# Attention: four max columns turned by one matmul, and the sinks' product in FP32r on a rounded and a remainder row

## What is computed

```python
def forgetting_attention(q, k, v, f_logit):
    ...
        s = jnp.einsum('bhqd,bhkd->bhqk', qb, kh) * scale
        s = s + cb[..., None] - cum[:, :, None, :]
        s = jnp.where(causal, s, -jnp.inf)
        p = jax.nn.softmax(s, axis=-1)
        return jnp.einsum('bhqk,bhkd->bhqd', p, vh)

def sliding_window_sink_attention(q, k, v, sinks):
    ...
    s = jnp.where(mask, s, -jnp.inf)
    # sink: each head's learned logit, broadcast to s.shape[:-1] + (1,)
    p = jax.nn.softmax(jnp.concatenate([s, sink], axis=-1), axis=-1)[..., :-1]
    out = jnp.einsum('bnhgqs,bnshd->bnqhgd', p, vv)
```

## Time and profile before

| what | value |
|---|---|
| median of 3 runs | 3542.21 us (3535.03 to 3544.0) |
| span of the profiled execution, first to last instruction | 3534.2 us |
| TensorE busy | 3215.7 us, 91% |
| VectorE busy | 2204.2 us, 62% |
| ScalarE busy | 1407.9 us, 40% |
| mean granted TensorE clock | 0.961 |

### The profile page before, as it was taken

The page is one execution under the profiler, slowest core; times in us unless marked ns, Lnnn a source line. Parts: engine busy times, 40 slices in busy tenths (PEclk is TensorE's granted clock), DMA queues, the critical chain, the costliest instruction groups (busy, mean ns, idle before and its releaser), DMA issues. The chain is left out here.

```text
span 3534.2 us, 43584 instructions
## 1 busy us (share of the span) xinstructions
PE 3215.7 (91%) x15232; PEld 2466.9 (70%) x15232; DVE 2204.2 (62%) x4305; ACT 1407.9 (40%) x2383; POOL 895.6 (25%) x828
## 2 busy tenths in 40 slices
PE   4999999889999997997889999997896899999798
PEld 4799888656666665876667887886784566666576
DVE  7111011267767776332389998995773689998766
ACT  5000001134444445212258998342554233333454
POOL 0111111257455460000421333344231211211000
PEclk9999999899999998998899999998998899999999
DMA  5322223466555533436311335364133523422444
GB/s 208 105 82 73 86 83 118 127 137 144 120 130 114 115 83 118 133 122 236 79 42 44 101 110 175 107 174 157 72 115 116 163 57 70 97 62 54 130 147 134
DMA packets 331916, 400.80 MB, mean 113 GB/s; under 512 B 100324, under 2 KB 249188, under 8 KB 319124
## 3 DMA queue, kind: packets, MB, share of 16 engines
q1 hardware_dynamic: 260376, 299.09, 29.7%
q10 hardware_dynamic: 67488, 78.03, 7.2%
q0 software_dynamic: 3840, 20.98, 2.5%
HBM read 265.39 MB, written 132.62 MB: 113 GB/s over the span
## 5 line engine op out<-in xcount | busy, mean ns | idle before, releaser
L2229 PE MATMUL f_pO<-f_PT,f_vv 128*128 128x512 f32 (+3 forms) x944 | 377.2, 481 | 19.7 <-ACT f_PT L2259 19.7
L2259 ACT ACTIVATE f_PT<-f_pS 128x512 f32<-128x512 f32 (+3 forms) x472 | 221.2, 472 | 325.3 <-PE f_pS L2197 152.8
L2890 DVE TENSOR_SCALAR_CACHE_REDUCE sharedI<-xI,TI 128x768 bf16<-128x768 f32 (+10 forms) x276 | 339.5, 1296 | 5.4 <-DVE TI L2896 5.2
L2694 PE MATMUL cbank<-hT_high,cw_hi 128*128 128x512 f32 x800 | 319.7, 400 | 19.9 <-DVE cw_lo L2849 6.8
L2259 ACT ACTIVATE n_PT<-n_pS 128x512 f32<-128x512 f32 (+4 forms) x352 | 176.6, 504 | 363.0 <-PE n_pS L2209 199.2
L583 PE MATMUL p_bank<-hT_high,p_w_hi 128*128 128x512 f32 (+1 forms) x768 | 304.9, 397 | 16.1 <-DVE p_w_lo L706 16.1
L2694 PE MATMUL cbank<-hT_low,cw_hi 128*128 128x512 f32 x800 | 316.7, 396 | 0.0
L2694 PE MATMUL cbank<-hT_high,cw_lo 128*128 128x512 f32 x800 | 316.3, 395 | 0.0
L2229 PE MATMUL n_pO<-n_PT,n_vv 128*128 128x512 f32 (+4 forms) x704 | 308.3, 519 | 0.0
L583 PE MATMUL p_bank<-hT_low,p_w_hi 128*128 128x512 f32 (+1 forms) x768 | 303.6, 395 | 0.0
L583 PE MATMUL p_bank<-hT_high,p_w_lo 128*128 128x512 f32 (+1 forms) x768 | 302.7, 394 | 0.0
(11 more groups left out here) (421 smaller groups left out, 7412.9 us busy)
## 6 DMA issues: line engine op xcount, KB each, us to landing
f_zz<-scratch_z ACTq DMA_DIRECT2D x128, 128.0 KB, 3.1
c_w_first<-in_w_in_dram SPq DMA_DIRECT2D x26, 512.0 KB, 4.5
cw_raw<-in_w_in_dram SPq DMA_DIRECT2D x25, 512.0 KB, 4.4
p_w_raw<-in_w_in_dram SPq DMA_DIRECT2D x22, 512.0 KB, 3.8
lent<-scratch_qkb POOLq DMA_DIRECT2D x40, 256.0 KB, 10.3
scratch_z<-p_stage ACTq DMA_DIRECT2D x32, 256.0 KB, 2.4
scratch_qk_high<-p_stage ACTq DMA_DIRECT2D x32, 256.0 KB, 2.6
scratch_qk_low<-p_stage_low ACTq DMA_DIRECT2D x32, 256.0 KB, 3.2
```

Of the source, the lines that this page charges most:

```text
L2229: pe.matmul(pO[:, B % 2, c0:c1], lhsT=vv[0:nk, b, kt, :], rhs=PT[0:nk, u % PR, c0:c1], start=(kt == 0 and not heads[h].local), stop=(heads ...
L2259: act.activation(PT[0:nk, u % PR, c0:c1], pS[0:nk, u % SR, c0:c1], ACT.Exp, scale=0.125).then_inc(s_ex, 1)
L2694: last = pe.matmul(bank[:, p % RING, 0:wd], lhsT=w_part[pw][b][:, c, :], rhs=rhs, start=(c == 0 and a == 0), stop=(c == DC - 1 and a == 2))
L2890: own_.up(v.tensor_scalar(junk_v[:, own_.at % 2, 0:(i + 1) * P], scores(i), T[:, j:j + 1], None, compare, ALU.add, accum_out=count[:, j:j ...
```

## The change

The four max columns go into one 128x128 tile, columns 0, 32, 64 and 96, so that one matmul turns them, onto partitions 0, 32, 64 and 96. ScalarE then moves four rows of 128 to row 96 of `QA`, from one partition each, instead of one piece of 32 partitions.

The sink's product becomes FP32r. So that no digits are lost, ScalarE computes the exponential twice, once in full FP32 (`es_full`) and once rounded (`es`, row 96), a new VectorE instruction, `sink_remainder`, writes the difference of the two to row 64 of `es`, and `only` has ones in rows 64 and 96. VectorE waits for ScalarE's pair, and the sink's product waits for VectorE.

```diff
-        Mx = m.sb(n_("Mx"), [P, 4, P], F32R)
+        Mx = m.sb(n_("Mx"), [P, P], F32R)
+        Mx_columns = Mx[:].rearrange("p (r c) -> p r c", r=4)[:, :, 0]
...
-            es = m.sb(n_("es"), [P, 2, QB4])
-            only = m.sb(n_("only"), [P, P])
+            es = m.sb(n_("es"), [P, 2, QB4], F32R)
+            es_full = m.sb(n_("esfull"), [P, QB4])
+            only = m.sb(n_("only"), [P, P], F32R)
...
+                step(gp.memset(only[64:65, HD:P].bitcast(F32), 1.0))
...
-                for r in range(4):
-                    last = pe.matmul(pR[:, r], lhsT=Mx[:, r], rhs=ident_r[:], start=True, stop=True)
-                last.then_inc(s_tr, 1)
+                pe.matmul(pR[:, 0], lhsT=Mx[:], rhs=ident_r[:], start=True, stop=True).then_inc(s_tr, 1)
...
-                act.activation(QA[h % NB][96:P, j * QB4:(j + 1) * QB4], pR[96:P].rearrange("p a b -> p (a b)"), ACT.Copy
-                               ).then_inc(s_mr, 1)
+                for r in range(4):
+                    at = j * QB4 + r * P
+                    last = act.activation(QA[h % NB][96:97, at:at + P], pR[32 * r:32 * r + 1, 0], ACT.Copy)
+                last.then_inc(s_mr, 1)
...
+                    if n:
+                        act.wait_ge(s_es, n)
                     act.wait_ge(s_mr, B + 1)
-                    act.activation(es[96:P, n % 2], QA[h % NB][96:P, j * QB4:(j + 1) * QB4].bitcast(F32), ACT.Exp,
-                                   bias=snk[96:P, heads[h].sink:heads[h].sink + 1], scale=-0.125).then_inc(s_es, 1)
+                    top = QA[h % NB][96:97, j * QB4:(j + 1) * QB4].bitcast(F32)
+                    for to in (es_full[96:97], es[96:97, n % 2]):
+                        last = act.activation(to, top, ACT.Exp, bias=snk[96:97, heads[h].sink:heads[h].sink + 1], scale=-0.125)
+                    last.then_inc(s_eh, 1)
...
+            def sink_remainder(B):
+                n = sink_no[B]
+                v.wait_ge(s_eh, n + 1)
+                v.tensor_tensor(es[64:65, n % 2], es_full[96:97], es[96:97, n % 2].bitcast(F32), ALU.subtract).then_inc(s_es, 1)
...
+                if u in sw.unit0[:-1] and sw.unit0.index(u) in sink_no:
+                    sink_remainder(sw.unit0.index(u))
```

More of the change, by code:

```diff
@@ L1858, in stage_attend @@
             s_snk = m.sem(n_("sinks_loaded"))
-            s_es = m.sem(n_("sink_exponentials"))
+            s_eh, s_es = m.sem(n_("sink_exponentials")), m.sem(n_("sink_remainders"))
         lower, upper = slice(0, HD), slice(HD, P)
@@ L2011, in _ @@
             if local_no:
-                step(gp.memset(es[:], 0.0))
-                step(gp.memset(only[:], 0.0))
-                step(gp.memset(only[96:97, HD:P], 1.0))
+                step(gp.memset(es[:].bitcast(F32), 0.0))
+                step(gp.memset(only[:].bitcast(F32), 0.0))
+                step(gp.memset(only[64:65, HD:P].bitcast(F32), 1.0))
+                step(gp.memset(only[96:97, HD:P].bitcast(F32), 1.0))
             gp.sem_inc(s_const, 1)
@@ L2353, in max_columns @@
                     n = sink_no[B]
-                    own_.up(v.tensor_tensor(Mx[:, :, 96], mxc[:, B % 2, :, 0],
+                    own_.up(v.tensor_tensor(Mx_columns, mxc[:, B % 2, :, 0],
                                             snk8[:, heads[h].sink:heads[h].sink + 1].to_broadcast([P, 4]), ALU.max))
@@ L2361, in max_columns @@
                     a, b = min(r for r, p in runs if p == n), max(r for r, p in runs if p == n) + 1
-                    last = v.tensor_reduce(Mx[:, a:b, 96], mxc[:, B % 2, a:b, 0:n], AX.X, ALU.max)
+                    last = v.tensor_reduce(Mx_columns[:, a:b], mxc[:, B % 2, a:b, 0:n], AX.X, ALU.max)
                 last.then_inc(s_stat, 1)
+            def sink_remainder(B):
+                n = sink_no[B]
+                v.wait_ge(s_eh, n + 1)
+                v.tensor_tensor(es[64:65, n % 2], es_full[96:97], es[96:97, n % 2].bitcast(F32), ALU.subtract).then_inc(s_es, 1)
             def weight(B):
```

## The result

The changed kernel takes 3550.03 us (median of 6 runs, 3548.7 to 3555.68), beside it the kernel before 3541.72 us (6 runs, 3533.82 to 3544.0): ratio 1.0027, with an interval of 1.0015 to 1.0039. It is slower by 5 to 14 us. The forecast was 3541; the range 3528 to 3556 holds the result, but the forecast said no change that can be told, and there is one. One of the 12 executions of the kernel of experiment 10 took 10096.54 us, the other 11 took 3528 to 3544; it is in no ratio.

What follows compares the result with a forecast made beforehand. TensorE and VectorE were taken to set the pace by turns, with GpSimd's loads and a late gate ending VectorE's half. Terms -14.8 - 5.0 + 4.1 + 9.5 + 4.8 = -1.4 us on 3542.2 gave 3541, range 3528 to 3556.

Steps and rivals of the forecast that it cites:

- What bounds the kernel: Both attentions: TensorE and VectorE set the pace in turn, VectorE in local heads, beside a chain of GpSimd and its loads.
- The turn: One turning matmul for four saves 0.36 us where TensorE sets the pace: 14.8 us in first attention, 5.0 in second.
- Copies and FP32r product at nothing: Four small ScalarE copies per block are covered, and the sink's faster product lies in VectorE stretches: both counted 0.
- The remainder's price: VectorE's subtraction in local heads: 0.69 us alone, 1.3 beside GpSimd; three of a head's four beside it, 4.6 us in all.
- each pair loses between 1.4 and 2.5 us; I take 1.9: Five later local-plus-plain head pairs of the first attention: remainders partly absorbed by idle time and slack, +9.5 us in all.
- nothing is absorbed: Far end for the five pairs: each loses the full 4.1 us of remainders, 20.5 us in all.
- The first local head: First attention's first local head, with no late gate behind it: remainders cost +4.1 us.
- The tail: Last two local heads: seven remainders in the chain without GpSimd, +4.8 us, at most 8 if ScalarE's pair is late.
- The clock: TensorE's granted clock, 1.00 in both halves of a pair's period; a fall there would show the prediction wrong.
- The sinks' three terms: Remainder costs in the first attention: first local head +4.1, five pairs +9.5, last two heads +4.8 us.
- the first rival: Whole kernel: turn's gain and remainders' cost cancel, within 10.6 us of before, bounds -13 to +16; chance 0.66.
- the third's: Rival: VectorE's stretch becomes each pair's longer chain; slower once a remainder costs over 0.95 us, up to +22, 3564; chance 0.15.

Runs made afterwards that it cites:

- experiment 10: Changed kernel with GpSimd's raw loads in the five pairs waiting until the plain head's first gate has landed; ratio 0.998 to the kernel before, 3534 us.
- experiments 1 and 3: Kernel before with only the one-matmul turn and small copies, 0.9922; that kernel plus FP32r sink product on rounded exponentials without remainder, 0.9934 (ratios to before).
- experiment 7: Changed kernel with the sink's two exponentials asked for two steps earlier, remainder where it was; ratio 1.0027 to the kernel before.

## Why the prediction was wrong

- **What bounds the kernel**: right in the main. VectorE sets the pace in every local head. In the third pair's local head it is busy 28.69 of 29.47 us after the change, 23.59 of 24.60 with the turn alone. Here are these two, then the same head before, and with the sink's change alone:

```profile
1007.61:1037.08 29.47, 22.45 (x122) 16.32 (x120) 28.69 (x59) 15.69 (x42) 26.90 (x38) 1.00 0.44 99
```

```profile
997.80:1022.40 24.60, 22.88 (x125) 16.86 (x124) 23.59 (x55) 14.29 (x39) 23.65 (x34) 1.00 0.45 110
```

```profile
1001.94:1027.51 25.57, 23.33 (x131) 17.46 (x130) 24.55 (x55) 12.96 (x29) 24.62 (x37) 1.00 0.45 103
```

```profile
1016.84:1046.09 29.25, 23.47 (x129) 17.25 (x127) 28.45 (x61) 14.47 (x32) 26.80 (x38) 1.00 0.44 100
```

- **The turn** (-14.8 and -5.0, -19.8 together): about right by size, not by place. By the ratios it is -16.6 beside the sinks, -19.1 with the gate out of the way and -27.6 (-23 to -32) alone. By the traces the second attention gave 3.6 us on average. The first gave 8.3 alone, 10.2 with the gate out of the way and 16.5 beside the sinks, half of the 10.2 in the pairs' local heads, where none was counted. Why these differ so much is not shown; in the turn-alone trace three plain heads were at the lower clock and gained nothing.
- **Copies and FP32r product at nothing**: right as far as can be told (experiments 1 and 3).
- **The remainder's price**: 28.3 us in all. The forecast's prices were 0.69 alone and 1.3 beside GpSimd; in a pair one of four was long, not three (0.71, 0.69, 1.39, 0.69: 3.5 us, where 4.6 was forecast). What was missed is that work put in between also moves its neighbours to other moments of GpSimd's work. In the third pair's local head the products of `finish` take 1.31 us with the turn alone and 2.50 after:

```profile
997.80:1022.40 24.60, 1.31 (x3) 1.00 0.45 110
```

```profile
1007.61:1037.08 29.47, 2.50 (x3) 1.00 0.44 99
```

So 3.5 us of remainders and 1.2 of `finish` make up the 4.5 that a local head grew by, within 0.2. Before, `finish` took 2.3 us there: its length depends on what of GpSimd's it falls beside, so that each move of the steps changes it, that of a one-input maximum too (1.81 us).
- **The step that failed**: "each pair loses between 1.4 and 2.5 us; I take 1.9". The VectorE time was meant to be half absorbed by the wait for the gate, which was taken for a chain of GpSimd's own. Against the turn alone a local head is 4.5 us longer (29.3 against 24.8) and its plain head gives back 0.5: 4.0 a pair, 20 us in five, where the forecast had 9.5. It is the end of the range that said "nothing is absorbed", 20.5. In the period looked at it isn't absorbed because the gate's request waits for VectorE's work: the request came 4.5 us later and the landing 3.0. A pair's period is 89.2 us, not the 85 to 86 of before that was to stay. Experiment 10 shows that the cost stays when the gate is punctual. No run moved the request alone, so this reading rests on the code and the traces.
- **The first local head** (+4.1): 33.4 against 25.9 with the turn alone, +7.5. Its remainders were 1.41, 1.66, 0.79 and 1.60 us, 2.7 over the bare length. Idle work without waits costs 6.4 there. The last 1.1 us are waits or the clock, which was 0.74 in this head after the change and 1.00 with the idle work; no run separates them.
- **The tail** (+4.8, at most 8): +8.1 against the turn alone. Idle work costs 4.9, the term as forecast; the rest is VectorE's wait for ScalarE's pair, which was given as the far end and taken as 0: experiment 7 takes it away and gets 3.6 us back. In the last head four remainders waited 0.6 to 1.4 us, and its blocks take 5.6 to 6.1 us where 4.8 was forecast. Here is VectorE ahead of its last remainder, which ScalarE's pair held up by 1.13 us:

```profile
1406.26 1.76 DVE L2393 RECIPROCAL f_w<-f_w 128x128 f32<-128x128 f32 x2
1409.15 0.69 DVE L2375 TENSOR_TENSOR f_es<-f_esfull,f_es 1x512 fp32r<-1x512 f32 x1 [1.13 <-ACT f_es L2296]
```
- **The clock**, whose fall was given as a sign of being wrong, fell in five of the six local heads of the pairs, to 0.74 to 0.94. In the five late pairs it doesn't explain their length: the head at 0.82 takes 29.0 us, the one at 1.00 takes 29.5. In the first pair it may.

The sinks' three terms were 18.4 us together. They measured 7.5, 20.0 and 8.1; with 0.4 given back in the first pair's plain head and 0.9 that lie ahead of all remainders, that is the 34.3 between the two kernels' ends. The time itself, 8 us over before by the medians, is inside the first rival's band. The mechanism is the third's, VectorE's stretch as the longer chain, with its threshold of 0.95 us a remainder: 34.3 / 32 is 1.07. With 34.3 for the remainders and the forecast's 19.8 for the turn the change would be at +14.5. By the ratios the turn alone took off 27.6 and the sinks' change then added 37.2, which leaves it near +9.

That the whole missed by 9 us only, and not by 22 as the first attention did in the traces, is luck: 6 us came back in the untouched part between the attentions, and the profile of before stood 8 us under its median where that of after stands 2.5 under.

## What to carry over

When an operation is added to the engine that sets the pace, count it in full. Idle time at the end of the stretch absorbs it only if what ends that idle time is asked for by another engine's chain: look up where the late transfer is *issued*, and what that issue waits for, not only where it lands. The two-input VectorE operation of 512 columns took 0.69 us on one partition as on 128, and up to 1.66 beside a working GpSimd; one idle instruction put in its place, without its waits, gave nine tenths of its price in one run. And a small load on the critical path should not be queued beside a large one that has time: here one wait ahead of the large loads was worth more than the change under study.

## What the runs showed of the hardware

- TensorE's clock fell in the changed kernel's local heads, most in the first (0.74). In one of them, the first of the four windows of 3 us shows TensorE busy 1.23, and the next two show the granted clock at 0.50 and 0.52, the 1.2 GHz level, and then 1.00 again. In the stretches of the earlier trace rows before, the clock was 1.00.

```profile
1203.00:1206.00 3.00, 1.23 (x6) 1.08 (x7) 2.97 (x4) 0.81 (x2) 3.00 (x3) 0.84 0.00 0
1206.00:1209.00 3.00, 3.00 (x12) 2.54 (x12) 2.88 (x9) 1.45 (x5) 2.43 (x4) 0.50 0.63 136
1209.00:1212.00 3.00, 3.00 (x13) 2.54 (x12) 2.94 (x6) 1.88 (x4) 2.71 (x6) 0.52 1.24 255
1212.00:1215.00 3.00, 3.00 (x22) 2.64 (x21) 2.82 (x8) 0.77 (x2) 0.00 (x0) 1.00 1.01 213
```

  VectorE is busy 2.8 to 2.97 of 3 us through all four, so the slower TensorE seems to cost little: the local head with the sink's change alone is as long (29.25 us) at a clock of 1.00. That it costs nothing was not tried by itself. In the plain heads, where TensorE sets the pace, a mean clock of 0.97 went with some 2 us more (57.99 and 59.97 us in the turn alone).
- The FP32r sink product is listed at 505 ns, two FP32 passes before at some 595 each. The saving on TensorE is real and bought no time.
- Runs of the kernel before spread over 3532 to 3555 us, and the part between the attentions, the same in all kernels, over 1331 to 1344 us. The times go with the mean granted clock: of 78 executions of before, the eight at 0.958 or less took 3545 to 3555 us, the eight at 0.963 or more 3532 to 3540. What makes the clock differ from one execution to the next was not found.
